# Reading the state-space inputs back on two transfer queues, and asking for one weight column earlier

## The chip, the core and the metric

The kernel runs on one core of a Trainium2 chip. The metric is the device time of one launch in microseconds (us). TensorE (PE in the profile) multiplies matrices, VectorE (DVE) and ScalarE (ACT) do element-wise work, GpSimd (POOL) a few fills, and SyncE (SP) issues most transfers (DMAs). A transfer that is issued from SP goes into SP's queue (q1 in the profile), one that is issued from ACT into ACT's queue (q10). All of them are carried by the same 16 DMA engines.

## The reference, cut to what matters

The program runs two blocks one after the other on a sequence of 1024 positions with 1024 channels. The change lies in the second block, in its state-space part:

```python
h = rms_norm(x, pre_g)
proj = jnp.einsum("bld,de->ble", h, w_in)
conv_in, z_c, u_s, z_s, g_c, g_s = jnp.split(proj, IN_OFFSETS, axis=-1)
...
y = jax.nn.gelu(s5_mimo(u_s, lam_re, lam_im, log_dt, b_re, b_im, c_re, c_im, d))
...
# s5_mimo: per group g of 16 channels, a complex state of 64 numbers
#   s_t = Abar s_{t-1} + Bbar u_t,   y_t = Re(C s_t) + D * u_t
```

`u_s` has 512 channels, that is 32 groups of 16.

## The kernel before, in words

The second block starts with a stretch in which TensorE normalises the input and makes four columns of `u_s` (names `u0` to `u3` in the code, 128 channels each), then the eight gate columns `zc0` to `zc7`. Each such column takes one 512 KB weight transfer into one of four slots of the buffer `ring`, and 16 logical 128x512 products. These column products stand at line L2095 for TensorE, whatever column they make.

The state-space part is cut into 128 blocks of 8 positions (`BLK` = 8, `NBLK` = 128) and takes these steps:

- ScalarE copies each `u` column into `u_perm` (L2367), and SP stores it to DRAM as `u_scratch` (`store_u`, L1979).
- VectorE makes powers of the state's matrix; its step `kernel` (L2678) is the last of the convolution kernel within a block. TensorE makes the kernel's products in two halves (`kernel`, L2142), with half of `zc0` between them.
- SP copies the kernel into place with eight SBUF to SBUF transfers, 32 KB to 256 KB each, which fill `K_lift` (L2003, `s_arena<-yT` in the profile; `K_placed` is their semaphore).
- TensorE turns the input matrix B (`flip_B`, L2148) with half of `zc1` between, and ScalarE places it (`place_B`, L2386).
- SP reads `u_scratch` back in another layout, with eight transfers of 256 KB (L2009, `yT<-u_scratch`, the code's `u_blk`; semaphore `u_loaded`). Transfer t of the eight writes 16 partitions.
- TensorE forms the inputs of the state from `u_blk` for the first half of the groups (`drive(0)`, L2157), then makes the column `zc3` and half of `zc4`, then reads the states out (`read_out(0)`, L2169 and L2173). The same follows for the other half (`drive(1)`, `read_out(1)`).
- Between `drive(0)` and `read_out(0)`, VectorE runs the recurrence over the 128 blocks, whose last step is `s0` (L2732).

Ahead of the recurrence VectorE needs a table of rotations (`turn_re`, `turn_im`). It is built by doubling (L2690 to L2702, with helper lines L2561 to L2566), followed by a copy of the decay (L2706). The first line of that table waits for `K_placed`, because the table's temporary space lies where the kernel lay before it was placed. `read_out` waits for `K_placed` too, and for `s0`.

All order is written out by hand: each engine's instruction list is the code's order, and SP's list is the order in which its queue gets transfers. An instruction in a list waits for its semaphores and holds up all behind it. In SP's list the weights of `zc2` are asked for behind the eight kernel placements. A weight transfer waits, ahead of its issue, until the column that used the slot before is done: for `zc2` that is `zc0`, for `zc3` it is `zc1`. TensorE makes `zc2` between `flip_B(1)` and `drive(0)`, and `zc3` behind `drive(0)`.

ScalarE's list in that stretch is `kernel0`, `kernel1`, the SiLU of `zc0` (L2373), `place_B(0)`, `place_B(1)`, then the SiLU of `zc1`, `zc2` and `zc3`, and `take_y(0)` (L2393). Behind the state-space part come the 31-tap convolution on VectorE beside more column products, and an output product at the end.

Of the kernel before, what the change touches and what calls it, by code (L numbers as in the profile page):

```python
# [30 lines left out]
GH = 16  # L31
BLK = P // GH
# [28 lines left out]
def block_program(nc, a, out):  # L61
# [3 lines left out]
    with ctx:  # L65
        def sem(name):
            return ctx.enter_context(nc.semaphore(name))
# [20 lines left out]
        def pair(n):  # L88
            return bank[:, 2 * n:2 * n + 2, :].rearrange("p a c -> p (a c)")
# [14 lines left out]
        def columns(w, n, kt=KT):  # L104

            return w.rearrange("(k p) c -> p k c", p=P)[:, :, bass.ts(n, P)]
# [1729 lines left out]
        w_in = a["w_in_2"][0]  # L1836
        CA, CB, ZC, ZS, GC, GS = (c // P for c in (0, D, 2 * D, 3 * D + 512, 4 * D, 5 * D))
        u_dram = nc.dram_tensor("u_scratch", (ST * P, BLK, NBLK), F32, kind="Internal").ap()
# [3 lines left out]
        with ExitStack() as scope:  # L1842
# [16 lines left out]
            u_blk = flat[:, 0:4096].rearrange("p (g k) -> p g k", g=GROUPS)  # L1859
# [47 lines left out]
            POST_BANKS = [(0, 1, 6), (2, 3, 7)]  # L1907

            u_stored = [sem("u_stored0"), sem("u_stored1")]
            K_placed, u_loaded = sem("K_placed"), sem("u_loaded")  # L1910
            y_stored, y_loaded = sem("y_stored"), sem("y_loaded")
            post_loaded, x_loaded2, out_stored = sem("post_loaded"), sem("x_again_loaded"), sem("out_stored")
            pad_zero = sem("conv_pad_zero")
# [54 lines left out]
            with nc.Block() as block:  # L1968
                @block.sync
                def _(sp):  # L1970
                    def load(name, w, n, kt=KT):

                        slot, _, freed = SLOT[name]
                        pe_b.wait(sp, freed)
                        sp.dma_start(ring[:, slot, 0:kt, :], columns(w, n)).then_inc(w_loaded[slot], 16)

                    def store_u(b):
                        act_b.wait(sp, f"u{b}")
                        sp.dma_start(u_dram[b * P:(b + 1) * P], u_perm[:, b % 2, :, :]).then_inc(u_stored[b % 2], 16)  # L1979
# [16 lines left out]
                    store_u(1)  # L1996
                    store_u(2)
                    store_u(3)

                    dve_b.wait(sp, "kernel")  # L2000
                    pool_b.wait(sp, "zero")
                    for r in range(BLK):
                        sp.dma_start(K_lift[r * GH:(r + 1) * GH, :, (BLK - 1 - r) * GH:], kernel16[:, :, 0:(r + 1) * GH]).then_inc(K_placed, 16)  # L2003
                    load("zc2", w_in, ZC + 2)
                    pe_b.wait(sp, "B_flip1")
                    for p in range(2):
                        sp.wait_ge(u_stored[p], 32)
                    for t in range(BLK):
                        sp.dma_start(u_blk[(BLK - 1 - t) * GH:(BLK - t) * GH, :, :],  # L2009
                                     u_dram.rearrange("(g h) t k -> t h g k", h=GH)[t]).then_inc(u_loaded, 16)  # L2010
                    load("zc3", w_in, ZC + 3)
# [71 lines left out]
                def _(pe):  # L2083
# [68 lines left out]
                    def drive(h):  # L2152
                        for x in range(2):
                            for jl in range(HP):
                                for g in range(2):
                                    j = h * HP + jl
                                    last = nc.tensor.matmul(bank[g * NS:(g + 1) * NS, 4 + 2 * x + jl // 4, (jl % 4) * P:(jl % 4 + 1) * P],  # L2157
                                                            B_lift[:, x, j, g * NS:(g + 1) * NS], u_blk[:, 2 * j + g, :], start=True, stop=True)
                        pe_b.mark(last, f"w{h}")
# [91 lines left out]
                    finish(tile)  # L2251
                    finish(early("zc2"))
                    act_b.wait(pe, "B1")
                    pe.wait_ge(u_loaded, BLK * 16)
                    drive(0)
                    finish(early("zc3"))
                    tile = early("zc4")
# [102 lines left out]
                def _(act):  # L2360
# [8 lines left out]
                    def silu_c(n):  # L2369
                        pe_b.wait(act, f"zc{n}")  # L2370
                        if n == 6:
                            dve_b.wait(act, "s1")
                        act_b.mark(act.activation(silu_zc[:, n, :], pair(PAIR[f"zc{n}"]), ACT.Silu), f"zc{n}")  # L2373
# [10 lines left out]
                    def place_B(x):  # L2384
                        pe_b.wait(act, f"B_flip{x}")
                        act_b.mark(act.activation(B_lift[:, x, :, :].rearrange("p j c -> p (j c)"), bank[:, 4:8, :].rearrange("p b c -> p (b c)"),  # L2386
                                                  ACT.Copy), f"B{x}")
# [78 lines left out]
                    silu_c(0)  # L2466
                    place_B(0)
                    place_B(1)
                    silu_c(1)
                    silu_c(2)  # L2470
                    silu_c(3)
# [64 lines left out]
                    for m in range(TT // 2):  # L2536
# [9 lines left out]
                        t = 2 * m + 1  # L2546
# [391 lines left out]
```

## Time and profile before

| | us |
|---|---|
| Median of 3 runs | 2266.24 |
| Lowest and highest of them | 2265.8 and 2268.85 |
| The profiled execution's own time | 2268.18 |
| Its span in the profile | 2266.1 |
| TensorE busy in it | 2176.8 (96%) |
| VectorE busy | 1311.4 (58%) |
| ScalarE busy | 593.0 (26%) |

The profiled execution lies within the three runs, 1.9 us above their median. The mean TensorE clock granted in it is 0.989 of full speed. TensorE is busy nearly throughout, so the places at which it stands still, or runs at a lower clock, are what a change of order can win or lose. The change lies at about 1335 to 1410 us of the span.

### The profile page before, as it was taken

Reading aid. Unit: us, or ns where it says so; the run is one execution under the profiler, and the core shown is the slowest. Engines: PE = TensorE matmul, PEld = TensorE weight load, DVE = VectorE, ACT = ScalarE, POOL = GpSimd, SP = SyncE. Lnnn points to the kernel's source line nnn. Section 1 sums busy time; section 2 is a strip of 40 time slices with the busy share of each in tenths; the row PEclk is TensorE's granted clock in tenths of the full one; section 3 lists DMA queues with packets and bytes.
Section 4 is the critical chain, followed back from the end, with each engine's and each line's share of the span. In section 5 each row is a group of like instructions: output and inputs, shape, how many; then the busy total and the mean of one; then the engine's idle time right before and its main releaser. Section 6 shows DMA issues by size and latency. Waiting matters only on the chain. (4 is left out here: it accounts for less than half of the span.)

```text
span 2266.1 us, 20611 instructions
## 1 busy us (share of the span) xinstructions
PE 2176.8 (96%) x7098; PEld 1120.0 (49%) x7098; DVE 1311.4 (58%) x1833; ACT 593.0 (26%) x960; POOL 172.3 (8%) x135
## 2 busy tenths in 40 slices
PE   6999999989999999999999999999999999999998
PEld 5444444346656656556454455544444444444443
DVE  4687733264664664764823676377469998341333
ACT  4355522233333443443213320121100000230012
POOL 0000000122212212211100000000000000000000
PEclk8999999999999999999999999999999999999999
DMA  9333420121111111111410344321111111015001
GB/s 324 114 110 116 130 103 0 74 65 37 34 26 43 29 33 39 35 32 38 130 32 19 121 64 59 78 76 33 42 33 47 33 33 47 28 37 197 26 19 56
DMA packets 200911, 146.86 MB, mean 65 GB/s; under 512 B 49997, under 2 KB 171906, under 8 KB 200834
## 3 DMA queue, kind: packets, MB, share of 16 engines
q1 hardware_dynamic: 186417, 144.14, 21.6%
q10 hardware_dynamic: 14048, 0.85, 0.4%
q0 software_dynamic: 384, 1.05, 0.2%
q8 instruction: 39, 0.64, 0.1%
q14 instruction: 23, 0.18, 0.0%
HBM read 126.45 MB, written 18.38 MB: 64 GB/s over the span
## 5 line engine op out<-in xcount | busy, mean ns | idle before, releaser
L2095 PE MATMUL bank<-hT,ring 128*128 128x512 f32 x1472 | 637.4, 594 | 2.5 <-DMA ring<-in_w_in 2.5
L2095 PEld LDWEIGHTS bank<-hT,ring 128*128 128x128 f32 x1472 | 279.6, 190 | 352.9 <-issue 349.2
L2756 DVE SCALAR_TENSOR_TENSOR yT<-s_arena,yT 128x1024 f32<-128x1024 f32 x240 | 308.3, 1285 | 8.4
L1235 PE MATMUL bank<-hT,ring 128*128 128x512 f32 x336 | 162.2, 595 | 1.8 <-ACT silu_z L1465 1.8
L2095 PE MATMUL bank<-yT,ring 128*128 128x512 f32 x256 | 110.0, 592 | 0.0
L1810 DVE SCALAR_TENSOR_TENSOR memory<-memory,col_exp_last,bank 128x128 f32<-128x128 f32 x64 | 22.2, 347 | 137.8 <-PE bank L1410 137.8
L2095 PE MATMUL bank<-ssm_y,ring 128*128 128x512 f32 x192 | 83.9, 592 | 0.6 <-DVE s_arena L2770 0.6
L1235 PE MATMUL bank<-resid,yT 128*128 128x512 f32 x168 | 82.5, 593 | 0.0
L2095 PEld LDWEIGHTS bank<-yT,ring 128*128 128x128 f32 x256 | 48.6, 190 | 61.2 <-issue 61.2
L1235 PEld LDWEIGHTS bank<-hT,ring 128*128 128x128 f32 x336 | 56.8, 193 | 36.1 <-issue 36.1
L2399 ACT ACTIVATE s_arena<-bank 128x1024 f32<-128x1024 f32 x8 | 8.2, 1023 | 242.5 <-PE bank L2095 242.5
L1773 DVE SCALAR_TENSOR_TENSOR buf_c<-bank,buf_c 128x512 f32<-128x512 f32 x32 | 22.1, 691 | 83.9 <-PE bank L1321 81.1
L2745 DVE TENSOR_TENSOR s_arena<-bank,s_arena 128x1024 f32<-128x1024 f32 x8 | 9.8, 1226 | 94.6 <-ACT s_arena L2399 94.6
L600 PE MATMUL bank<-hT,ring 128*128 128x512 f32 x144 | 63.4, 595 | 0.3 <-DVE lru_arena L825 0.3
L1305 PE MATMUL bank<-hT,yT 128*128 128x512 f32 x128 | 60.2, 593 | 0.0
L2827 DVE TENSOR_TENSOR s_arena<-bank,s_arena 128x1024 f32<-128x1024 f32 x8 | 9.8, 1224 | 86.3 <-PE bank L2095 86.3
L1532 ACT ACTIVATE delta<-bank,gdn_stat 128x128 f32<-128x128 f32 x64 | 23.5, 367 | 138.0 <-PE bank L1406 138.0
L2095 PEld LDWEIGHTS bank<-ssm_y,ring 128*128 128x128 f32 x192 | 36.4, 190 | 46.8 <-issue 46.8
L2324 PE MATMUL bank<-resid,s_arena 128*128 128x512 f32 x128 | 56.5, 593 | 1.1 <-DVE yT L2862 1.1
L645 PE MATMUL bank<-ada,yT 128*128 128x512 f32 x128 | 55.8, 593 | 0.7 <-issue 0.7
L645 PE MATMUL bank<-lru_arena,yT 128*128 128x512 f32 x128 | 56.1, 592 | 0.0
L1235 PE MATMUL bank<-resid,ring 128*128 128x512 f32 x112 | 53.8, 593 | 0.0
(533 smaller groups left out, 3354.4 us busy)
## 6 DMA issues: line engine op xcount, KB each, us to landing
ring<-in_w_in SPq DMA_DIRECT2D x48, 512.0 KB, 3.7
ada<-in_ada_w SPq DMA_DIRECT2D x8, 2048.0 KB, 8.0
ring<-in_gdn_in_w SPq DMA_DIRECT2D x32, 512.0 KB, 4.1
resid<-in_x SPq DMA_DIRECT2D x8, 1024.0 KB, 8.8
ring<-in_lru_in_w SPq DMA_DIRECT2D x16, 512.0 KB, 3.7
lru_arena<-in_ada_w SPq DMA_DIRECT2D x6, 1024.0 KB, 13.1
x_scratch<-resid SPq DMA_DIRECT2D x2, 2048.0 KB, 10.6
decayT<-g_scratch SPq DMA_DIRECT2D x8, 512.0 KB, 4.3
```

The lines of the kernel that those rows point to most:

```text
L600: last = nc.tensor.matmul(bank[:, to, :], w[:, k, :], v[:, k, :], start=(first and k == 0), stop=(k == KB - 1), skip_group_check=not (firs ...
L645: last = nc.tensor.matmul(bank[:, OUT_BANK[i], :], yT[:, k, t * P:(t + 1) * P], out_w[c][:, k, :], start=(k == 0), stop=(k == KT - 1))
L1235: last = nc.tensor.matmul(bank[:, to, :], w[:, k, :], v[:, k, :], start=(first and k == 0), stop=(k == KB - 1), skip_group_check=not only)
L1305: last = nc.tensor.matmul(bank[:, n % 4, :], yT[:, k, t * P:(t + 1) * P], w, start=(k == 0), stop=(k == KT - 2))
L1532: hd_act.mark(act.activation(delta[:, 1, :], R4[:, 4, :], ACT.Copy, scale=stat[:, 5, c:c + 1]), f"new{c}")
L1773: hd_dve.mark(dve.scalar_tensor_tensor(out=dst[:, half, :], in0=first[:, half, :], scalar=-1.0, in1=second[:, half, :], op0=ALU.mult, op1= ...
L1810: hd_dve.mark(dve.scalar_tensor_tensor(out=memory[:, :], in0=memory[:, :], scalar=cols["exp_last"][:, h, c:c + 1], in1=R5[:, 0, :], op0=AL ...
L2095: last = nc.tensor.matmul(bank[:, 2 * PAIR[name] + h, :], w[:, k, :], src[:, k, h * HALF:(h + 1) * HALF], start=(k == 0), stop=(k == kt - 1))
L2324: last = nc.tensor.matmul(bank[:, to, :], x[:, k, m, :], w[:, k, :], start=(start and k == 0), stop=(k == HK - 1), skip_group_check=not alone)
L2745: dve_b.mark(dve.tensor_tensor(padded[:, p, PAD:], pair(PAIR[f"a{n}"]), conv_sig[:, p, :], ALU.mult), f"cu{n}")
L2756: dve_b.mark(dve.scalar_tensor_tensor(out=yT[:, n, :], in0=padded[:, p, j:j + S], scalar=taps[:, p, j:j + 1], in1=yT[:, n, :], op0=ALU.mul ...
L2827: dve_b.mark(dve.tensor_tensor(sig_gc[:, n, :], pair(PAIR[f"co{n}"]), sig_gc[:, n, :], ALU.mult), f"gated{n}")
```

## The change

Three edits, two in SP's list and one in ScalarE's, with a semaphore of its own for the second queue:

```diff
-            K_placed, u_loaded = sem("K_placed"), sem("u_loaded")
+            K_placed, u_loaded, u_loaded_act = sem("K_placed"), sem("u_loaded"), sem("u_loaded_act")
...
                     store_u(3)
+                    load("zc2", w_in, ZC + 2)
 
                     dve_b.wait(sp, "kernel")
                     pool_b.wait(sp, "zero")
                     for r in range(BLK):
                         sp.dma_start(K_lift[r * GH:(r + 1) * GH, :, (BLK - 1 - r) * GH:], kernel16[:, :, 0:(r + 1) * GH]).then_inc(K_placed, 16)
-                    load("zc2", w_in, ZC + 2)
                     pe_b.wait(sp, "B_flip1")
                     for p in range(2):
                         sp.wait_ge(u_stored[p], 32)
-                    for t in range(BLK):
+                    for t in range(BLK // 2):
                         sp.dma_start(u_blk[(BLK - 1 - t) * GH:(BLK - t) * GH, :, :],
                                      u_dram.rearrange("(g h) t k -> t h g k", h=GH)[t]).then_inc(u_loaded, 16)
...
-                    pe.wait_ge(u_loaded, BLK * 16)
+                    pe.wait_ge(u_loaded, BLK // 2 * 16)
+                    pe.wait_ge(u_loaded_act, BLK // 2 * 16)
                     drive(0)
...
                     place_B(0)
                     place_B(1)
+                    for p in range(2):
+                        act.wait_ge(u_stored[p], 32)
+                    for t in range(BLK // 2, BLK):
+                        act.dma_start(u_blk[(BLK - 1 - t) * GH:(BLK - t) * GH, :, :],
+                                      u_dram.rearrange("(g h) t k -> t h g k", h=GH)[t]).then_inc(u_loaded_act, 16)
                     silu_c(1)
```

SP's list of the kernel before, from the stores of `u` (`u_scratch<-s_arena`) over the eight placements of the kernel (`s_arena<-yT`) to the weights of `zc3` to `zc5`:

```order
116 L1979 DMA u_scratch<-s_arena 128x1024 x3
117 L2003 DMA s_arena<-yT 16x32x16
118 L2003 DMA s_arena<-yT 16x32x32
119 L2003 DMA s_arena<-yT 16x32x48
120 L2003 DMA s_arena<-yT 16x32x64
121 L2003 DMA s_arena<-yT 16x32x80
122 L2003 DMA s_arena<-yT 16x32x96
123 L2003 DMA s_arena<-yT 16x32x112
124 L2003 DMA s_arena<-yT 16x4096
125 L1975 DMA ring<-in_w_in 128x8x128
126 L2009 DMA yT<-u_scratch 16x32x128 x8
127 L1975 DMA ring<-in_w_in 128x8x128 x3
```

The same stretch of SP's list in the changed kernel:

```order
116 L1979 DMA u_scratch<-s_arena 128x1024 x3
117 L1975 DMA ring<-in_w_in 128x8x128
118 L2004 DMA s_arena<-yT 16x32x16
119 L2004 DMA s_arena<-yT 16x32x32
120 L2004 DMA s_arena<-yT 16x32x48
121 L2004 DMA s_arena<-yT 16x32x64
122 L2004 DMA s_arena<-yT 16x32x80
123 L2004 DMA s_arena<-yT 16x32x96
124 L2004 DMA s_arena<-yT 16x32x112
125 L2004 DMA s_arena<-yT 16x4096
126 L2009 DMA yT<-u_scratch 16x32x128 x4
127 L1975 DMA ring<-in_w_in 128x8x128 x3
```

The weights of `zc2` (row 125 before) stand ahead of the eight placements now (row 117), and four of the eight read-backs are gone from this list.

ScalarE's list of the kernel before, from the copies of `u` over the two placements of B (L2386) to the SiLU of `zc1` to `zc3` (L2373 x3) and `take_y(0)` (L2393):

```order
383 L2367 ACTIVATE s_arena<-bank 128x1024 x4
384 L2381 ACTIVATE yT<-bank 16x2x1024 x2
385 L2373 ACT_TABLE_LOAD
386 L2373 ACTIVATE resid<-bank 128x1024
387 L2386 ACTIVATE s_arena<-bank 128x2048 x2
388 L2373 ACTIVATE resid<-bank 128x1024 x3
389 L2393 ACTIVATE ssm_y<-bank 128x2048
```

And in the changed kernel, with line numbers one higher:

```order
383 L2368 ACTIVATE s_arena<-bank 128x1024 x4
384 L2382 ACTIVATE yT<-bank 16x2x1024 x2
385 L2374 ACT_TABLE_LOAD
386 L2374 ACTIVATE resid<-bank 128x1024
387 L2387 ACTIVATE s_arena<-bank 128x2048 x2
388 L2473 DMA yT<-u_scratch 16x32x128 x4
389 L2374 ACTIVATE resid<-bank 128x1024 x3
```

The four read-backs stand between the placements of B and the SiLU of `zc1`. TensorE's and VectorE's lists hold the same instructions in the same order as before; only TensorE's wait ahead of `drive(0)` looks at two semaphores.

## Rows read from the trace of the kernel before

**Rows 1.** The page, the chain that ended last, by engine and by line

```profile
PE bank L2095 34%; PE bank L2324 4%; DVE yT L2756 1%; DMA yT<-u_scratch 1%; PE bank L2215 1%; PE bank L2207 1%; SPq L2009 1%; PE bank L2173 0%; PE bank L2169 0%; DVE resid L2573 0%; PE bank L2157 0%; PE bank L2142 0%; ACT ssm_y L2429 0%; ACT ssm_y L2431 0%; ACT hT L2440 0%
```

**Rows 2.** TensorE's timeline: start us, us, instructions, in brackets idle before and releaser

```profile
1329.64 7.13 PE L2095 MATMUL bank<-hT,ring 128*128 128x512 f32 x16
...
1346.97 7.03 PE L2095 MATMUL bank<-hT,ring 128*128 128x512 f32 x16
1356.50 15.47 PE L2095 MATMUL bank<-hT,ring 128*128 128x512 f32 x32 [2.49 <-DMA ring<-in_w_in]
1375.07 3.71 PE L2157 MATMUL bank<-yT,s_arena 128*64 128x128 f32 x64 [3.10 <-DMA yT<-u_scratch]
1378.71 20.87 PE L2095 MATMUL bank<-hT,ring 128*128 128x512 f32 x48
1399.42 0.61 PE L2169 MATMUL bank<-yT,s_arena 128*128 128x128 f32 x4
```

**Rows 3.** VectorE's timeline: table begins, recurrence begins, s0

```profile
1351.30 0.18 DVE L2690 TENSOR_SCALAR resid<-gate_b 128x16 f32<-128x16 f32 x1 [11.72 <-issue]
...
1379.90 1.22 DVE L2718 TENSOR_TENSOR yT<-bank,resid 128x1024 f32<-128x1024 f32 x1
...
1397.75 1.22 DVE L2732 TENSOR_TENSOR s_arena<-yT 128x1024 f32<-128x1024 f32 x1
```

**Rows 4.** SP's queue, its issues in order of time

```profile
1335.65 9.49 SPq L2003 DMA_DIRECT2D s_arena<-yT  x8
1345.19 2.29 SPq L1975 DMA_DIRECT2D ring<-in_w_in  x1
1347.59 15.52 SPq L2009 DMA_DIRECT2D yT<-u_scratch  x8
1363.16 29.95 SPq L1975 DMA_DIRECT2D ring<-in_w_in  x3
```

**Rows 5.** Landings: eight kernel placements, eight read-backs, one undisturbed weight transfer

```profile
L2003 SPq DMA_DIRECT2D s_arena<-yT x8: 615/880/1884, 1335.6 to 1343.6; - x8
DMA to landing us min/median/max: 2.3/5.3/7.7
...
L2009 SPq DMA_DIRECT2D yT<-u_scratch x8: 507/2164/3077, 1347.6 to 1360.9; - x8
DMA to landing us min/median/max: 9.7/12.5/14.0
...
L1975 SPq DMA_DIRECT2D ring<-in_w_in x1: 368/368/368, 1392.7 to 1392.7; - x1
DMA to landing us min/median/max: 3.8/3.8/3.8
```

**Rows 6.** Waits of TensorE from 1480 us to the end, all of them

```profile
PE bank L2324 <- DVE yT L2862: 1.1, 1, 1.1
PE bank L2095 <- DVE s_arena L2770: 0.6, 1, 0.6
```

**Rows 7.** ScalarE's timeline, the second placement of B

```profile
1347.17 1.88 ACT L2386 ACTIVATE s_arena<-bank 128x2048 f32<-128x2048 f32 x1 [6.23 <-PE bank L2148]
```

**Rows 8.** Stretches: length, busy by engine, granted clock, DMA share, GB/s

```profile
1349.80:1351.20 1.40, 1.40 (x4) 0.57 (x3) 0.00 (x0) 0.00 (x0) 0.00 (x0) 1.00 0.90 262
1352.00:1374.00 22.00, 17.47 (x37) 7.20 (x35) 20.15 (x85) 2.05 (x2) 0.00 (x0) 0.92 1.26 114
1356.00:1360.00 4.00, 3.50 (x5) 1.69 (x6) 3.56 (x21) 0.00 (x0) 0.00 (x0) 0.57 1.26 110
```

**Rows 9.** TensorE's timeline in block one: small products undisturbed, and behind a wait

```profile
509.65 1.04 PE L1326 MATMUL bank<-ident,cv 128*128 128x128 f32 x8
...
511.38 1.95 PE L1321 MATMUL bank<-baseT,prod 128*128 128x128 f32 x16
...
592.36 3.75 PE L1321 MATMUL bank<-base,part 128*128 128x128 f32 x16 [3.05 <-DMA base<-x_scratch]
595.90 1.92 PE L1326 MATMUL bank<-ident,cv 128*128 128x128 f32 x8
```

## The prediction, as it was put on record before the changed kernel ran

> **What bounds the kernel now.** I read the page's chain first: the product columns of line L2095 alone are 34% of it, and the read-backs of `u_scratch` appear with 1% for their issue and 1% for their flight [rows 1]. So TensorE sets the end, apart from a few gaps, and one of them is ours. The list of TensorE's waits says the same of all that follows: from 1480 us to the end it waits only twice, for 1.1 and 0.6 us, and both times for VectorE [rows 6]. Nothing behind our stretch can soak up a delay in it, and a gain in it reaches the end whole.
>
> TensorE's timeline of the stretch shows two gaps. `zc1` ends at 1346.97 + 7.03 = 1354.00, and `zc2` starts at 1356.50, after 2.49 us of waiting for its weights. `zc2` ends at 1371.97, and `drive(0)` starts at 1375.07, after 3.10 us of waiting for the read-backs [rows 2]. Between the two, 32 matmuls take 15.47 us, while 48 of the same shape take 20.87 us later, that is 0.435 us each or 13.9 us for 32. The missing 1.57 us are clock: from 1356 to 1360 the granted clock averages 0.57, that is mostly the 1.2 GHz level, after the stop at 1354 [rows 8]. Both gaps and the slow clock cost 2.49 + 3.10 + 1.57 = 7.16 us. This is what the change aims at.
>
> Then VectorE's timeline, since TensorE needs `s0` for `read_out(0)`. VectorE stands still for 11.72 us and begins its rotation table at 1351.30. From there to the end of `s0` at 1397.75 + 1.22 = 1398.97 it is 47.67 us without a gap worth naming: the products with `drive(0)`'s result begin at 1379.90, and `drive(0)` had ended at 1378.78, so even that is no wait [rows 2, 3]. TensorE starts `read_out(0)` at 1399.42 [rows 2], right behind its column work and only 0.45 us after `s0`. So two chains meet there, almost level. TensorE's has 7.16 us to give. VectorE's has nothing.
>
> What started VectorE's chain? The view names no releaser ("issue"), but the code makes that first line wait for `K_placed`, and the landings give the time: the eighth placement was issued at 1343.6 and landed 7.7 us later, at 1351.3 [rows 3, 5]. VectorE's chain starts with the landing of the kernel's placement.
>
> **The change, part by part.**
>
> *The weights of `zc2` ahead of the placements.* Before, they were asked for at 1345.19, behind the eight placements [rows 4]. Now their issue waits for the end of `zc0`, 1329.64 + 7.13 = 1336.77 [rows 2]. An undisturbed weight transfer takes 0.37 us to issue and lands after 3.8 us [rows 5], so they land at about 1340.6, and `zc2` starts at 1354.00: minus 2.49 and minus 1.57 on TensorE's own chain. But the placements were issued from 1335.65 on [rows 4], and now can't start before 1336.77 + 0.37 = 1337.14. Their issue moves by 1.5 us. Their transfers queue behind the weights in the same queue: the first landed at 1335.65 + 2.3 = 1337.95 before [rows 5], and now lands a little after 1340.6, which is 2.65 us and more later. The placements ran without pause, eight landings between 1337.95 and 1351.3, one each 1.9 us, so a late start passes to the last. I take 2.9 us; the ends are 1.5 (only the issue moves, the queue closes up again) and 2.9.
>
> *Four read-backs on ScalarE's queue.* ScalarE finishes the second placement of B at 1347.17 + 1.88 = 1349.05 [rows 7] and issues from there; SP begins its four behind the placements, where it began at 1347.59 before [rows 4]. The kernel's last placement would now land at 1351.3 + 2.9 = 1354.2. For 5.1 us the ScalarE transfers are on the same 16 engines with it. If engines took turns evenly, that tail would take twice as long, +5.1; if there is room, 0. There is some: the read-backs move 114 GB/s although weights move 262 GB/s through the same engines [rows 8]. I take 0.5, nearer to 0 since a transfer needs about a microsecond to start and the last placement is one contiguous row for each partition. So `K_placed` is late by 2.9 + 0.5 = 3.4 us, ends 1.5 and 8.0.
>
> ScalarE itself: behind its four issues stands the SiLU of `zc1`. One read-back takes 0.5 to 3.1 us to issue [rows 5], so four take 2 to 12 us, and the SiLU ends by 1362 instead of about 1355. Who waits for it is `zc3`, behind `drive(0)`, after 1371. That is hidden. If the cover were gone, each us of it would stand in front of `zc3`.
>
> *When the read-backs are all in.* The last landed at 1360.92 + 14.0 = 1374.9 before [rows 5]. The eight need the queue for some 22 us at 114 GB/s [rows 8]. Does a second queue make them faster? The row: at 114 GB/s the DMA share is 1.26, at 262 GB/s it is 0.90, so here packets are slow and not many, which leaves open whether a second queue adds packets in flight. The Trainium skill ("DMA: Bandwidth & Descriptors", section "Issuing engines are not separate DMA queues") says that all queues run on the same 16 engines and interleave, and that a second issuing engine saves only issue time. By that rule `drive(0)` would start at about 1373 to 1375, by the other reading at 1368. The sum is the same by both, which is the point of the next part.
>
> *What TensorE's gain is worth.* VectorE's chain starts at 1351.30 + 3.4 and takes 47.67 us as long as `drive(0)` ends before 1379.90 + 3.4 = 1383.3, which holds even if the read-backs are no faster (1378.8). So `s0` ends at 1402.4. Without its gaps TensorE would stand ready at 1399.42 - 7.16 = 1392.26, and must wait. `read_out(0)` starts about 0.1 us after `s0`, at 1402.5, which is 3.1 us later than before. The 7.16 us don't vanish: they become one wait of up to 10 us, or two if the read-backs stay slow, in front of `read_out(0)`.
>
> *The clock behind that wait.* Stops of this size are not free of it. In block one, after 3.05 us of waiting, 16 small products take 3.75 us against 1.95 undisturbed, and the next 8 take 1.92 against 1.04 [rows 9]: 2.7 us lost. After the wait ahead of `zc2` it was 1.57, and after the 3.10 us ahead of `drive(0)` nothing visible. I take 1.5, ends 0 and 2.7.
>
> *Sum:* 3.4 late placement, -0.3 since `s0` was ahead by 0.45 and a release costs about 0.1, +1.5 clock = +4.6 us. The profiled execution (2268.18) becomes 2272.8. It lies 1.9 above the median of the runs shown, and it is the median that is to be met: 2266.24 + 4.6 = 2270.8. Ends of the sum: 1.5 - 0.3 + 0 = +1.2 and 8.0 - 0.3 + 2.7 = +10.4. About 0.2%, or 4.5 us, is what a measurement of this kernel can tell from no change; the forecast lies on that line.
>
> **The rivals.**
>
> *Little delay, no clock loss (not slower).* The queue closes up, the placement is 1.5 to 2.5 us late, and `read_out(0)` restarts at full clock. For it: the wait ahead of `drive(0)` cost no clock, and the first placements (32 and 64 KB) wait on their issue more than on engines. Against it: the wait here is longer than any of those above. Time: +1.2 to +2.2, so 2267.9.
>
> *The placement isn't VectorE's starter (faster).* If the 11.72 us had another end, or the placement caught up wholly, `s0` would stay at 1398.97; TensorE still could not pass it, so the gain is at most 0.35 us. For 7.16 us and 2259.1, VectorE's chain would have to be 7 us earlier or `read_out(0)` not to wait for it. Only a misreading of that row would do it. The landing at 1351.3 and the start at 1351.30 speak against it.
>
> *The two queues share the engines evenly (slower by more).* The tail of the placements is stretched by ScalarE's transfers by 2.5 to 5.1 us instead of 0.5. `s0` is late by 5.4 to 8. It decides from the point at which `K_placed` lands after 1355.7. Time: +6.6 to +9, about 2274. For it: the queues meet for the whole tail. Against it: the room in the rates above. The same rule of the skill, interleaving on the same 16 engines, speaks for this one.
>
> **Chances.** Forecast case (2.6 to 4.0 late, clock loss of 1 to 2): 0.55. It lies across the 0.2% line, a little over half of it within. Little delay: 0.22. Even sharing: 0.18. Faster by the full gain: 0.05. So faster 0.05, within 0.2% 0.22 + 0.29 = 0.51, slower 0.26 + 0.18 = 0.44. The range goes from 2267.0, just under the lower end of the sum, to 2275.5: it leaves out the faster case and the upper part of even sharing.
>
> **What would show it.** In the profile of the changed kernel: no wait in front of `zc2`, and full clock in it; the first line of VectorE's table at about 1354.7 instead of 1351.30, right at the last placement's landing; `s0` 47.7 us later; a wait of TensorE for VectorE in front of `read_out(0)`, 4 to 10 us, which was not there; then some microseconds at the lower clock; and from there all as before, shifted. I am wrong if `read_out(0)` starts before 1399, if VectorE's table starts before 1352.8 or after 1358, or if it is `drive(0)` that comes so late that VectorE waits for it.

## The result, and the profile after

| | before | changed |
|---|---|---|
| Median of 8 runs each, us | 2269.39 | 2279.49 |
| Lowest and highest, us | 2265.8 and 2277.27 | 2269.62 and 2281.27 |
| Profiled execution's own time, us | 2268.18 | 2277.2 |
| Mean granted TensorE clock in it | 0.989 | 0.985 |

The ratio of the times is 1.0038, with a 95% interval of 1.0026 to 1.005: slower by about 8.6 us (5.9 to 11). The direction was forecast and the size was not: 4.6 us were expected, and 2279.49 lies outside the range, whose upper end was 2275.5. Part of the distance isn't the change's: the kernel before has a median of 2269.39 over eight runs, 3.1 us more than the 2266.24 of the three runs that the forecast was added to.

TensorE's timeline of the changed kernel (start, length, instructions, idle time before and its releaser) answers to [rows 2]:

```profile
1340.14 7.03 PE L2095 MATMUL bank<-hT,ring 128*128 128x512 f32 x16
...
1348.76 20.77 PE L2095 MATMUL bank<-hT,ring 128*128 128x512 f32 x48
1369.45 3.71 PE L2157 MATMUL bank<-yT,s_arena 128*64 128x128 f32 x64
1373.10 20.87 PE L2095 MATMUL bank<-hT,ring 128*128 128x512 f32 x48
1403.00 1.22 PE L2169 MATMUL bank<-yT,s_arena 128*128 128x128 f32 x4 [9.04 <-DVE s_arena L2738]
1404.15 1.23 PE L2173 MATMUL bank<-s_arena 64*128 64x128 f32 x8
...
1417.04 0.71 PE L2173 MATMUL bank<-s_arena 64*128 64x128 f32 x8
...
1418.98 7.13 PE L2095 MATMUL bank<-hT,ring 128*128 128x512 f32 x16
```

Both old waits are gone: `zc1`'s second half, `zc2` and `drive(0)` stand end to end. A new wait of 9.04 us for VectorE's `s0` stands ahead of `read_out(0)`. The read-out itself then takes 1418.98 - 1403.00 = 15.98 us, against 10.19 before (from 1399.42 to 1409.61 in that trace). Its groups of products take 1.22 and 1.23 us, and only near the end 0.71. The stretches of the changed kernel show the clock (length, busy time by engine, granted clock, DMA share, GB/s):

```profile
1354.00:1364.00 10.00, 10.00 (x25) 4.47 (x24) 7.73 (x48) 1.02 (x1) 0.00 (x0) 1.00 1.24 149
...
1399.00:1403.00 4.00, 0.00 (x0) 0.00 (x0) 3.88 (x4) 0.00 (x0) 0.00 (x0) 0.50 0.00 0
1403.00:1415.00 12.00, 12.00 (x62) 9.76 (x63) 0.00 (x0) 0.00 (x0) 0.00 (x0) 0.50 0.00 0
1416.00:1419.00 3.00, 3.00 (x33) 2.40 (x31) 0.00 (x0) 0.00 (x0) 0.00 (x0) 1.00 0.02 5
```

TensorE works for twelve microseconds at 0.50, its 1.2 GHz level, before it is given 2.4 GHz again.

VectorE's timeline of the changed kernel, the lines that answer to [rows 3]: start of the table, start of the recurrence, last step of `s0`.

```profile
1355.25 0.18 DVE L2696 TENSOR_SCALAR resid<-gate_b 128x16 f32<-128x16 f32 x1 [13.84 <-DMA s_arena<-yT]
...
1383.86 1.23 DVE L2724 TENSOR_TENSOR yT<-bank,resid 128x1024 f32<-128x1024 f32 x1
...
1401.72 1.22 DVE L2738 TENSOR_TENSOR s_arena<-yT 128x1024 f32<-128x1024 f32 x1
```

This time the view names the releaser: the placement of the kernel. The chain from there to the end of `s0` is 47.69 us long (47.67 before).

The two traces are compared from the start of `zc1`'s first half, at 1338.36 before and 1340.14 after, since 1.78 us of the difference had arisen far ahead of the change. Counted from there:

| | before | changed | moved by |
|---|---|---|---|
| VectorE's table begins | 12.94 | 15.11 | +2.17 |
| `drive(0)` begins | 36.71 | 29.31 | -7.40 |
| `read_out(0)` begins | 61.06 | 62.86 | +1.80 |
| `read_out(0)` is done | 71.25 | 78.84 | +7.59 |

The spans of the two profiles differ by 2275.4 - 2266.1 = 9.3 us (their device times by 9.02), of which 1.78 come from before the stretch and 7.59 from it. Behind it the two waits of [rows 6] stand as they stood, 1.1 and 0.6 us.

The queues of the changed kernel, SP's first, ScalarE's last, answer to [rows 4]:

```profile
1338.59 0.38 SPq L1975 DMA_DIRECT2D ring<-in_w_in  x1
1339.07 10.82 SPq L2004 DMA_DIRECT2D s_arena<-yT  x8
1350.01 4.69 SPq L2009 DMA_DIRECT2D yT<-u_scratch  x4
...
1349.02 5.42 ACTq L2473 DMA_DIRECT2D yT<-u_scratch  x4
```

The weights go out when `zc0` ends, and the placements start 1.64 us later than before, counted from `zc1`'s start. ScalarE's four issues end at 1354.44, before `zc1` does at 1355.79, so the SiLU behind them isn't late, where up to 7 us were allowed for.

### The profile page after: what moved, and what is told of

Read it like the earlier page. It is cut to its first block and busy times, and to the rows that moved or that the text cites. A ratio compares the mean times of both kernels' runs of the same rounds, so it can differ in the third digit from the quotient of the medians.

```text
span 2275.4 us, 20612 instructions
## 1 busy us (share of the span) xinstructions
PE 2181.7 (96%) x7098; PEld 1124.3 (49%) x7098; DVE 1311.7 (58%) x1833; ACT 593.3 (26%) x960; POOL 172.3 (8%) x135
```

## The experiments

Theory A has two terms. The placement of the kernel is late, and through VectorE's chain so is `s0`. The wait this makes for TensorE lets its clock fall, and the read-out's small products don't bring it back. Each run below has its own profile and is timed beside runs of the kernel before. A profile shows one execution, and executions of one kernel differ, so times are compared by the table and mechanisms by the profiles.

| run | median us | before beside it | ratio (95% interval) |
|---|---|---|---|
| weights ahead only | 2270.3 | 2269.63 | 1.001 (0.9994 to 1.0027) |
| split only | 2268.26 | 2269.63 | 0.9989 (0.9974 to 1.0003) |
| wait filled with idle products | 2271.89 | 2269.63 | 1.0009 (0.9994 to 1.0025) |
| table's space moved, both edits | 2262.03 | 2269.63 | 0.9955 (0.9937 to 0.9973) |
| changed kernel again | 2280.89 | 2268.61 | 1.0054 (1.0041 to 1.0067) |
| column products behind the wait | 2274.03 | 2268.61 | 1.0027 (1.0017 to 1.0036) |
| half a column inside the wait | 2264.05 | 2268.61 | 0.9986 (0.9974 to 0.9997) |
| table's space and weights, no split | 2267.98 | 2268.61 | 0.9997 (0.9988 to 1.0006) |
| table's space only | 2268.93 | 2269.02 | 0.9996 (0.9986 to 1.0007) |
| table's space moved, both edits, again | 2260.73 | 2269.02 | 0.9966 (0.9953 to 0.9979) |

**One edit alone: the weights of `zc2` ahead.**

```diff
 # kernel before
                     store_u(3)
+                    load("zc2", w_in, ZC + 2)
...
                         sp.dma_start(K_lift[r * GH:(r + 1) * GH, :, (BLK - 1 - r) * GH:], kernel16[:, :, 0:(r + 1) * GH]).then_inc(K_placed, 16)
-                    load("zc2", w_in, ZC + 2)
```

> Only the weights of zc2 are asked for ahead of the kernel's placements; all eight read-backs stay on SP's queue. Theory A (the late start of VectorE's table delays s0 by about 2 us, and the wait of TensorE ahead of read_out(0) then lets the clock fall, which the small products of the read-out do not bring back): the table starts 1.5 to 2.5 us later than before; drive(0) still waits 3 to 6 us for the read-backs, so the wait ahead of read_out(0) is short, 2 to 4 us. Time +2 us where the clock stays up, +4 to +8 us where it falls. Rival B (the loss comes from the second queue, which disturbs the placements and everything behind): no second queue here, so 0 to -4 us. Rival C (only the late placement counts, the clock is a side effect worth 1 to 2 us): +3 us.

TensorE's timeline and one stretch of this run:

```profile
1337.19 7.03 PE L2095 MATMUL bank<-hT,ring 128*128 128x512 f32 x16
...
1372.72 5.12 PE L2157 MATMUL bank<-yT,s_arena 128*64 128x128 f32 x64 [6.15 <-DMA yT<-u_scratch]
...
1400.82 0.71 PE L2169 MATMUL bank<-yT,s_arena 128*128 128x128 f32 x4 [2.18 <-DVE s_arena L2732]
```
```profile
1350.00:1366.00 16.00, 16.00 (x39) 7.03 (x37) 11.59 (x64) 1.02 (x1) 0.00 (x0) 1.00 1.21 106
```

The landings of the eight placements (L2004) in this run:

```profile
DMA to landing us min/median/max: 3.4/6.1/8.4
```

VectorE's table begins at 1353.04, or 15.85 from `zc1`'s start: 2.91 later than before, and no earlier than in the first profile of the changed kernel. So the weights in front of the placements make a delay of this size without any second queue. Whether the second queue adds to it is seen further down, in the second profile of the changed kernel. `drive(0)` waits 6.15 us, which leaves 2.18 for the wait ahead of the read-out, and in this execution the read-out ran at full clock and took 10.29 us. The median is +0.7 us only, and by the interval of the ratio the edit lies anywhere between -1.4 and +6.1 us. Of the 12 runs, eight lie between 2268.5 and 2273.3 at a mean clock of 0.988 or 0.989, and four between 2277.7 and 2279.9 at 0.984 or 0.985.

**The other edit alone: the split.**

```diff
 # changed kernel
                     store_u(3)
-                    load("zc2", w_in, ZC + 2)
...
                         sp.dma_start(K_lift[r * GH:(r + 1) * GH, :, (BLK - 1 - r) * GH:], kernel16[:, :, 0:(r + 1) * GH]).then_inc(K_placed, 16)
+                    load("zc2", w_in, ZC + 2)
```

> Only the read-backs are split over the two queues; the weights of zc2 stay behind the placements. Theory A: the table starts within 1 us of before, zc2 still waits 2.5 us; drive(0) does not wait any more, so 3.1 us of TensorE's chain turn into a wait of 3 to 4 us ahead of read_out(0) for s0. Time 0 to +1 us where the clock stays up, +3 to +7 us where it falls in that wait. Rival B: the placement is late by 2 us or more here too and the time is +5 to +10 us as in the changed kernel. Rival C: within 1 us of before, whatever the clock.

TensorE's timeline of this run:

```profile
1340.84 7.03 PE L2095 MATMUL bank<-hT,ring 128*128 128x512 f32 x16
...
1360.22 15.70 PE L2095 MATMUL bank<-hT,ring 128*128 128x512 f32 x32 [3.74 <-DMA ring<-in_w_in]
1375.85 3.71 PE L2157 MATMUL bank<-yT,s_arena 128*64 128x128 f32 x64
...
1401.53 0.71 PE L2169 MATMUL bank<-yT,s_arena 128*128 128x128 f32 x4 [1.17 <-DVE s_arena L2738]
```

VectorE's table begins at 1353.77, 12.93 from `zc1`'s start, which is before's 12.94. With the split alone the second queue doesn't delay the placements, and rival B, which makes it the whole cause of the loss, is out. The wait ahead of `drive(0)` is gone, the one for the weights, beside which ScalarE's read-backs now run, is 1.25 us longer (3.74 against 2.49), and a wait of 1.17 us for `s0` appears, less than the 3 to 4 us I expected. `read_out(0)` begins at 60.69, 0.37 earlier than before: this is the 0.45 us by which `s0` was ahead, and all that TensorE could win.

**The wait filled with products that nobody reads.** Ten extra products are computed, and their result is overwritten. The profile counts two instructions for each.

```diff
 # changed kernel
                     next(tile)
+                    act_b.wait(pe, "zc3")
+                    for k in range(10):
+                        nc.tensor.matmul(bank[:, 2, :], ident[:, :], hT[:, k % KT, 0:HALF], start=True, stop=True)
                     dve_b.wait(pe, "s0")
```

> The changed kernel with ten products of 128x512 into a bank that nobody reads, placed in the wait ahead of read_out(0); they take 10 x 0.87 = 8.7 us of a wait of 9.04 us and their result is overwritten. They add work and remove none. Theory A: the clock stays at its upper level through the read-out, which takes 10.2 us instead of 16.0, and the time falls by 5 to 6 us against the changed kernel, to before +2 to +4 us. Rivals B and C: the read-out's length does not depend on it, time as in the changed kernel (+8 to +10 us over before) or longer.

TensorE's timeline of this run: the extra products, the first of the read-out, and what follows the read-out.

```profile
1393.62 8.75 PE L2262 MATMUL bank<-hT,ident 128*128 128x512 f32 x20
1403.16 0.71 PE L2169 MATMUL bank<-yT,s_arena 128*128 128x128 f32 x4 [0.80 <-DVE s_arena L2741]
...
1413.45 7.13 PE L2095 MATMUL bank<-hT,ring 128*128 128x512 f32 x16
```

With 8.75 us of useless work added, the read-out takes 10.29 us instead of 15.98. The run's ratio is 1.0009, where the changed kernel has 1.0038 and 1.0054, each against runs of before beside it. `read_out(0)` begins at 63.21 from `zc1`'s start, as in the changed kernel (62.86), so what the products changed is the clock of the read-out, and in these two profiles the clock is the larger term: 5.7 us of 7.59. Two of its 12 runs still took 2280.6 and 2282.5 us, at 0.986 and 0.985; I have no profile of such a run.

**The changed kernel once more.**

> The changed kernel itself once more, for its profile and its spread beside the others. Both theories: +8 to +10 us over before, a wait of about 9 us ahead of read_out(0), and the read-out at the lower clock for most of its length (16 us instead of 10.2) in most runs. If instead the profile shows the read-out at full clock, the slow read-out of the first profile was chance and theory A loses its larger term.

TensorE's timeline of this run: `drive(0)`, three groups of the read-out and its end.

```profile
1369.58 3.71 PE L2157 MATMUL bank<-yT,s_arena 128*64 128x128 f32 x64 [2.00 <-DMA yT<-u_scratch]
...
1403.06 1.22 PE L2169 MATMUL bank<-yT,s_arena 128*128 128x128 f32 x4 [8.96 <-DVE s_arena L2738]
...
1405.36 1.22 PE L2169 MATMUL bank<-yT,s_arena 128*128 128x128 f32 x4
...
1407.16 0.71 PE L2169 MATMUL bank<-yT,s_arena 128*128 128x128 f32 x4
...
1414.88 7.13 PE L2095 MATMUL bank<-hT,ring 128*128 128x512 f32 x16
```

VectorE's table, and the landings of the eight placements:

```profile
1355.30 0.18 DVE L2696 TENSOR_SCALAR resid<-gate_b 128x16 f32<-128x16 f32 x1 [15.85 <-DMA s_arena<-yT]
```
```profile
DMA to landing us min/median/max: 3.8/5.8/10.1
```

Two things differ from the first profile. `zc1` starts at 1338.20 here, so the table begins 17.10 us after it, 4.16 later than before and not 2.17: the last placement took 10.1 us to land instead of 8.4. Of the seven profiles with both edits (two of this kernel and five of versions made from it) three have 8.4 and four have 10.0 to 10.2; the two with the weights ahead and one queue have 8.4 and 8.5. So the second queue seems to stretch the last placement by 1.7 us in some executions and not at all in others; against the run with the weights alone the table begins 0.7 us earlier in the first profile and 1.3 later in this one. Two profiles with one queue are too few to call it shown. And the read-backs landed later, so that `drive(0)` waited 2.00 us for them.

The wait ahead of the read-out is nearly the same, 8.96 us, but here the clock came back after 3.4 us: the read-out takes 11.82 us, and this execution took 2273.11. The other four runs took 2279.4 to 2282.9 at 0.983 to 0.985. With the eight of the first timing, 11 of 13 runs of the changed kernel are of the long kind. The size of the loss is thus no constant: it differs from execution to execution, and mostly it is large. Where the time of the other four went no profile shows. As an estimate, a read-out that is at the lower clock throughout would take its 16 groups times the 1.15 us of the first profile, 18.4 us, or 8.2 more than before; with the late `s0` that is 10 to 12 us, which fits them.

**The same wait with large products right behind it.** Column `zc4`'s second half runs ahead of the read-out instead of behind it. The order of the step names in TensorE's list follows suit and is left out below.

```diff
 # changed kernel
                     next(tile)
                     dve_b.wait(pe, "s0")
                     pe.wait_ge(K_placed, BLK * 16)
-                    read_out(0)
                     finish(tile)
+                    read_out(0)
+                    tile = early("zc5")
+                    next(tile)
                     act_b.wait(pe, "y0")
                     drive(1)
-                    finish(early("zc5"))
+                    finish(tile)
```

> The changed kernel with the same wait for s0 at the same place, but with the second half of column zc4 right behind it and read_out(0) after that; half of zc5 fills the place ahead of drive(1). Same work, other order. Theory A (the wait lowers the clock, and the read-out's small products are what keeps it low): wait of 9 us as before, zc4's half at the lower clock for 3 to 7 us, then the read-out at full clock, 10.2 us: 3 to 5 us faster than the changed kernel. Rival D (the length of the wait sets how long the clock stays low, about 17 us, whatever follows): zc4's half takes about 14 us, and the time is that of the changed kernel within 1.5 us.

TensorE's timeline of this run, and two stretches of it:

```profile
1401.75 8.52 PE L2095 MATMUL bank<-hT,ring 128*128 128x512 f32 x16 [9.08 <-DVE s_arena L2740]
1410.11 0.61 PE L2169 MATMUL bank<-yT,s_arena 128*128 128x128 f32 x4
...
1420.30 7.13 PE L2095 MATMUL bank<-hT,ring 128*128 128x512 f32 x16
```
```profile
1401.80:1404.20 2.40, 2.40 (x3) 1.12 (x4) 0.00 (x0) 0.00 (x0) 0.00 (x0) 0.50 0.00 0
1404.60:1410.00 5.40, 5.40 (x14) 2.40 (x13) 0.00 (x0) 0.00 (x0) 0.00 (x0) 1.00 0.00 0
```

The wait is 9.08 us. The half column takes 8.52 us instead of 7.03 to 7.13, and the read-out behind it 10.19 us, at full clock: the two stretches show 0.50 at its start and 1.00 from 1404.6 on. The clock costs about 1.4 us here, and 5.8 and 1.6 in the two profiles of the changed kernel, with the same work and nearly the same wait. Rival D is out: the clock is back 2.8 us after TensorE resumes, and not at the end of some 17 us. The profiles alone would leave chance as a rival, since 1.6 is hardly more than 1.4. The times decide: 2274.03 against 2280.89 by the medians of nine and five runs side by side, more than the 3 to 5 us expected, and the two intervals of the ratio don't meet. The length of the wait doesn't set its price by itself; what stands behind it counts. Even so this version's median is 5.4 us over before, where its profile, counted from `zc1` and without the half column that it has more, is 3.1 us behind; that rest is open.

**Half a column inside the wait.** Here too the order of the step names follows suit and is left out.

```diff
 # changed kernel
-                    tile = early("zc4")
-                    next(tile)
+                    finish(early("zc4"))
                     dve_b.wait(pe, "s0")
                     pe.wait_ge(K_placed, BLK * 16)
                     read_out(0)
-                    finish(tile)
+                    tile = early("zc5")
+                    next(tile)
                     act_b.wait(pe, "y0")
                     drive(1)
-                    finish(early("zc5"))
+                    finish(tile)
```

> The changed kernel with the second half of zc4 ahead of the wait for s0, and half of zc5 behind the read-out. Same work, and 7.06 us of the 9.04 us wait are filled with useful products. Theory A: wait of about 2 us, the read-out at full clock in most runs, read_out(0) starts when it did in the changed kernel, and 7.06 us of work are already done: 12 to 13 us faster than the changed kernel, 4 to 6 us faster than before. Rival C (late placement alone, clock irrelevant): 7 us faster than the changed kernel, so 1 to 3 us slower than before.

TensorE's timeline of this run:

```profile
1373.04 27.73 PE L2095 MATMUL bank<-hT,ring 128*128 128x512 f32 x64
1403.78 0.71 PE L2169 MATMUL bank<-yT,s_arena 128*128 128x128 f32 x4 [3.01 <-DVE s_arena L2738]
1404.42 1.11 PE L2173 MATMUL bank<-s_arena 64*128 64x128 f32 x8
...
1417.09 7.13 PE L2095 MATMUL bank<-hT,ring 128*128 128x512 f32 x16
```

The median is 4.6 us under before, as expected, though the ratio says 3.2 us (0.7 to 5.9). The profile was one of the dearer executions (2268.45): even its rest of a wait, 3.01 us instead of the 2 expected, cost clock. The first products ran at full speed, the clock fell 0.8 us into the read-out and was back 6.8 us later, and the read-out took 13.3 us. Of its 11 runs eight lie between 2261.6 and 2266.6, so a shorter wait seems to cost less clock in most executions, but it can cost some.

**The cause of the wait removed.** VectorE's table gets its temporary space where `u_perm` lay, so it need not wait for the placements. The wait for the stores of `u`, which stood behind the table, moves ahead of it (its old place is left out below).

```diff
 # changed kernel
-                    dve.wait_ge(K_placed, BLK * 16)
                     pe_b.wait(dve, "u3")
                     dve.wait_ge(x_kept, 16 * TT)
+                    for p in range(2):
+                        dve.wait_ge(u_stored[p], 32)
+                    f1, f2 = (arena[:, SH_AT + n * 1024:SH_AT + (n + 1) * 1024] for n in range(2))
...
                     pool_b.wait(dve, "zero")
+                    dve.wait_ge(K_placed, BLK * 16)
                     for h in range(2):
```

> The changed kernel with the temporary space of VectorE's rotation table moved from where the kernel lay to where u_perm lay (free once the stores of u have landed), so that the table need not wait for the placements; the wait for K_placed now stands ahead of the recurrence. Theory A: the table starts some 14 us earlier, s0 is set by drive(0) and comes before TensorE has finished its column work, no wait ahead of read_out(0), full clock: 7 us faster than before, 16 us faster than the changed kernel. Rival B: the second queue's disturbance remains, +2 us or more over before. Rival C: -5 to -7 us as well; this run tells A and C from B only.

> The changed kernel with the table's space moved, once more beside the table's move alone. Theory A: -6 to -8 us against before. Rival E: the same as the run with the table's move alone.

VectorE's and TensorE's timelines of the first of the two runs:

```profile
1341.34 0.19 DVE L2698 TENSOR_SCALAR resid<-gate_b 128x16 f32<-128x16 f32 x1
...
1374.21 1.23 DVE L2725 TENSOR_TENSOR yT<-bank,resid 128x1024 f32<-128x1024 f32 x1 [4.26 <-PE bank L2157]
...
1392.07 1.22 DVE L2739 TENSOR_TENSOR s_arena<-yT 128x1024 f32<-128x1024 f32 x1
```
```profile
1370.36 3.71 PE L2157 MATMUL bank<-yT,s_arena 128*64 128x128 f32 x64 [0.93 <-issue]
1374.01 20.87 PE L2095 MATMUL bank<-hT,ring 128*128 128x512 f32 x48
1394.71 0.61 PE L2169 MATMUL bank<-yT,s_arena 128*128 128x128 f32 x4
```

The table begins 14 us earlier, and now VectorE waits for TensorE (4.26 us) and not the other way round. `s0` is done 1.4 us before TensorE reaches the read-out, which runs at full clock. Both runs beat both kernels: 2262.03 and 2260.73 us, 7.6 and 8.3 us under the medians of before. No run of the twelve lies above 2264.3. What is left on TensorE's path is `drive(0)`: it begins 0.93 us late here, when the last read-back lands (issued at 1353.7, at most 16.6 us to landing, that is 1370.3), and 1.39 us late in the second run.

**Parts of that version.** With the weights ahead and the table moved, but all read-backs on SP:

> The table's temporary space moved and the weights of zc2 ahead, but all eight read-backs on SP's queue (no split). It tells what the second queue is worth once VectorE's chain is out of the way. Theory A (the second queue makes the read-backs land earlier by 5 us, as in the changed kernel against the run with the weights alone): drive(0) waits 5 to 6 us, 5 us or more slower than with the split, about -2 us against before. Rival: the queues only interleave, the read-backs land at the same time, -6 us as with the split.

TensorE's timeline of this run, `drive(0)`:

```profile
1375.73 6.61 PE L2157 MATMUL bank<-yT,s_arena 128*64 128x128 f32 x64 [5.91 <-DMA yT<-u_scratch]
```

`drive(0)` waits 5.91 us and then runs slowly itself, 6.61 us instead of 3.71. The gain is all gone (ratio 0.9997, where about -2 us was expected). The median is 0.6 us under its own before, where the two runs with the split are 7.6 and 8.3 under theirs, so the second queue is worth 7 to 8 us by the medians and 7 to 9.5 by the ratios, once VectorE is out of the way. Some 3 us of that are the clock in `drive(0)`, and the rest is the wait. And the table's move alone, on the kernel before:

> The kernel before with nothing but the temporary space of VectorE's rotation table moved, so the table starts before the placements have landed. Theory A: TensorE's chain is the one that decides there, with its waits of 2.49 and 3.10 us for the two transfers, and s0 comes early for nothing: within 1 us of before. The 7 us of the earlier run with both changes are then the joint effect of freeing both chains. Rival E (moving the table's space is worth 7 us by itself): -5 us or more here.

TensorE's timeline of this run, `zc2` and `drive(0)`:

```profile
1355.71 14.00 PE L2095 MATMUL bank<-hT,ring 128*128 128x512 f32 x32 [2.87 <-DMA ring<-in_w_in]
1372.85 3.71 PE L2157 MATMUL bank<-yT,s_arena 128*64 128x128 f32 x64 [3.13 <-DMA yT<-u_scratch]
```

Both transfer waits are there, 2.87 and 3.13 us, and the ratio is 0.9996. Rival E is out. In this execution neither wait cost clock: `zc2` took 14.00 us, where it took 15.47 in the profile of the kernel before, behind a shorter wait. Its 12 runs spread from 2260.7 to 2272.3, and two of them are shorter than any of the 17 runs of before beside them (2265.6 to 2272.4); I don't know why.

## Why the prediction was wrong in size

None of the signs by which it called itself wrong came: the table, the wait and `read_out(0)` are where it put them. The path was right, one term was not.

- **Both chains meet at `read_out(0)`: right.** The 7.16 us of TensorE's chain became a wait of 9.04 us for `s0`, with the span of VectorE's chain as read, 47.69 us. The runs with the table's space moved show the other half: with VectorE's chain freed, the same two edits bring 7.6 and 8.3 us by the medians.
- **The late placement: right, with a spread that wasn't foreseen.** I took 2.9 for the queue and 0.5 for the second queue's contention, 3.4 in all. The two profiles of the changed kernel have 2.17 and 4.16, and the two runs with the weights ahead on one queue put the last landing 2.8 to 2.9 later. Of contention the last placement shows nothing in three profiles and about 1.7 us in four. With the -0.3 us for the margin (measured -0.4), `read_out(0)` came 1.80 and 3.80 us late where 3.1 were forecast.
- **The read-backs on two queues: left open, now settled in part.** The rule of the Trainium skill ("DMA: Bandwidth & Descriptors", section "Issuing engines are not separate DMA queues") that I weighed says queues interleave on the same engines and a second one saves only issue time. The landings say otherwise here, and the measurement decides. Counted from `zc1`'s start, `drive(0)` could begin at 29.31 and 31.38 in the two profiles of the changed kernel, and at 35.53 and 35.29 in the two runs with the weights ahead on one queue. In the stretches shown the engines moved 149 GB/s with two queues and 106 with one, at almost the same DMA share (1.24 and 1.21). Both stretches hold part of `zc3`'s weights, so these aren't rates of the read-backs alone, and the second profile of the changed kernel is lower, 129 GB/s from 1352 to 1366. My 22 us for the eight was the length of a stretch and no quotient: 8 x 256 KB at 114 GB/s is 18.4 us. The sum didn't use it.
- **The step that failed: "The clock behind that wait".** I put it at 1.5 us with 2.7 as the end, from three waits behind which either column products stood or small products for 3.7 and 5.3 us. It measured 5.8 us in the first profile, 1.6 in the second, and in most runs it was large, to judge by their times and mean clocks. What I didn't ask is what TensorE does after it resumes. The read-out is 10 us of small products on end, and they can run on at the lower clock for up to 13 us. The run with a half column behind the same wait (1.4 us lost) and the one with the wait filled (none lost in its profile) show it.
- With 5.8 in place of 1.5, 2.2 in place of 3.4 and -0.4, the sum is +7.6 us, which is what the first profile shows against before (7.59). The second has 1.6, 4.2 and -0.4, together 5.4, near the forecast. The medians are 10 and 12 us apart, more than either profile; that the rest is clock as well is an inference from the mean clocks (0.983 to 0.985 against about 0.989) and from no profile. One run of the eight took 2269.62 us at 0.989, which would fit a read-out at full clock.
- "Even sharing of the queues", the rival that gave about +8 us, came nearer in size, mainly by another mechanism: the tail of the placements was stretched by 0 to 1.7 us, not by 2.5 to 5.1.

## What to carry to other kernels

When a wait in front of TensorE goes, look for the other input that its next waiting instruction needs, and how long that one's chain is: here VectorE's was level with it to 0.45 us, so two good edits could win nothing until a third freed it. Price a new wait by what stands behind it: 9 us in front of large products cost 1.4 us of clock, and in front of a run of small products 1.6 in one profile and 5.8 in another, with most times on the dear side. And take the profile of a changed kernel twice before you call a small term zero. If a wait can't be removed, move large products into it or right behind it.

## What the runs showed of the hardware that I had not expected

- A run of small products (128x128, two thirds of the instructions on 64 rows) ran on at 1.2 GHz for 12.9 us without a stop between them in one execution, and for 3.4 us in another. Behind the same wait, column products of 128x512 were at 2.4 GHz after 2.8 us. The waits of 2.49 and 3.74 us ahead of `zc2` cost 1.6 and 1.8 us of clock in two profiles, and the one of 2.87 us none in a third.
- With a second transfer queue the eight read-backs were in 4 to 6 us earlier. ScalarE's four write partitions 0 to 63 and SP's four 64 to 127, so the two queues also write different halves at a time. No run alternates the halves in one queue, so whether the gain is the queue's or the order's is open.
- Some executions are 7 to 10 us longer than the rest at a mean clock of 0.984 or 0.985 instead of about 0.989. The kernel before does it too, in 1 of 8 runs and 4 of 30, and in none of 26 and of 17 in two other series; beside the 30, the weights alone did it in 4 of 12 and the split alone in 2 of 12. None was profiled but the first one of the changed kernel, so the place of that loss in the others is open.
